# Loads in halves, a norm in VectorE's gaps, and the residual's squares moved into the attention block

## The chip, the cores and the metric

The kernel runs on one core of a Trainium2 chip. The metric is the device time in microseconds (us); lower is better. A core has five engines that run side by side and wait for one another through semaphores: TensorE (PE, matmuls and transposes), VectorE (DVE), ScalarE (ACT), GpSimd (POOL) and SyncE (SP), which here only issues DMAs. TensorE reads SBUF and writes PSUM; the others take its results from PSUM.

## The reference

One inference step of a one-layer hybrid decoder, for a prompt of 512 tokens and 64 sample tokens (8 sequences of 8), so NT = 576 tokens of D = 1024 features, all in float32:

```
h = h + mixer(rmsnorm(h))          # gated delta rule (4 heads) beside a chunked spatial gate (4 groups)
h = h + mem_attend(rmsnorm(h))     # attention of 4 heads over 256 memory rows
h = h + peer(rmsnorm(h))           # 8 heads choose 16 of 16384 experts for each token
y = rmsnorm(h)
rmsnorm(x) = x * rsqrt(mean(x*x) + 1e-6) * g
```

The mixer projects the normalised tokens with `w_in` (1024 x 3080): q, k and v go through a causal convolution of four taps and SiLU, q and k are scaled to unit length; the value rows of the spatial gate (`gv`) go through GELU and a layer norm over the 128 channels of each of 4 groups; two columns per head give the gates beta and g = -exp(a_log) * softplus(a + dt_bias). The normalised value rows of the sample tokens are also an output.

## The kernel before

Activations lie feature-major: `hT` is 128 partitions x 8 slices k x 576 tokens, the residual. Weights come in tiles of 128 output columns (128 x 8 x 128). Each float32 product is made from three products of split operands: ScalarE copies the rounded high part of a weight tile (`split_high`, L194), POOL subtracts for the low part (`split_low`, L200), and TensorE runs 8 x 3 x 2 matmuls of 288 columns (`products`, L212). The program is a sequence of blocks; at a block's end all engines meet in a barrier. The order inside a block is the order in which each engine's instructions are written.

**Input block** (`mixer_inputs`). SyncE issues eight slices of `hT`, then the constants `cst`, gains and small weights and the first three weight tiles, on one queue. ScalarE squares the slices (L113), TensorE sums the squares over the partitions with a matrix of ones out of `cst` (L121), ScalarE takes the root (L129), VectorE the reciprocal (L136) and then the scaled slices (L138), which ScalarE and VectorE split. All six small loads share one semaphore, `loaded`. Then a list `ITEMS` sets the order on TensorE and ScalarE: 24 weight tiles, with eight `l2` items (sums of squares of q and k), the gates' small matmuls (`ab`) and transposes (`turn`) put between. At tile x ScalarE first splits tile x + 1 and then takes tile x out of PSUM. For each `l2` item VectorE runs a reciprocal and a scaling (L447, L448). After the eighth come the value rows' mean, difference, square and sum (L453 to L457, `ln_vars`), ScalarE's root (`ln_roots`), three passes over the value rows (L460 to L462, `ln_done`), and the gates' functions, which ScalarE takes up behind its last tile (L393 to L402). SyncE stores the sample's value rows and waits for that store.

**Attention block** (`memory_attention`). Its last part multiplies by `w_mo`: eight tiles, m = QUERY to 4*KT - 1; VectorE adds each tile to the residual (L1468, `added`).

**Expert-score block** (`peer_scores`). It begins with squares, sums, root and reciprocal over the new residual (L113, L121, L129, L136), then the scaled slices (L138) and their splits (L1709, L1710 on ScalarE, L1744, L1747 on VectorE), for which the first tile of `peer_wq` waits slice by slice.

Of the kernel before, what the change touches and what calls it, by code (L numbers as in the profile page):

```python
# [230 lines left out]
def mixer_inputs(nc, io, sem, hT, cst, gains, rows, ps, cT, zT, vv, gate):  # L231

    with ExitStack() as ctx:
# [18 lines left out]
        h_loaded, loaded = sem("in_h_loaded"), sem("in_loaded")  # L252
# [29 lines left out]
        def _(sp):  # L282
            for k in range(KT):
                sp.dma_start(hT[:, k, :], io["xT"][:, k, :]).then_inc(h_loaded, 16)
            sp.dma_start(cst[:, :], io["consts"]).then_inc(loaded, 16)
            sp.dma_start(gains[:, :], io["gains"]).then_inc(loaded, 16)
            sp.dma_start(wab[:, :, :], w_in[:, :, 2048:2056]).then_inc(loaded, 16)
            for m in range(3):
                tiles.load(sp, m, w_in[:, :, COLS[m]:COLS[m] + P])
            sp.dma_start(cw[:, :, :], io["conv_w"]).then_inc(loaded, 16)  # L290
# [17 lines left out]
        def _(pe):  # L308
            pe.wait_ge(loaded, 96)
# [6 lines left out]

# [22 lines left out]
        def _(act):  # L339
            chain = Chain(act, act_seq)  # L340
            act.wait_ge(h_loaded, 16 * KT)
            norm_squares(act, hT, nT, squares)
            act.wait_ge(loaded, 96)
# [4 lines left out]
            act.wait_ge(zeroed, 1)  # L348

# [8 lines left out]
            for i, (kind, x) in enumerate(ITEMS):  # L358
# [31 lines left out]
                if kind == "tile" and 1 <= x <= QKV_TILES:  # L390
                    silu(x - 1)
            act.wait_ge(ln_vars, 1)
            act.activation(st[:, 1, :], st[:, 1, :], ACT.Sqrt, bias=cst[:, C_EPS:C_EPS + 1],  # L393
                           scale=1.0 / P).then_inc(ln_roots, 1)

            act.wait_ge(gate_exp_in, 1)
            act.activation(gw[:, 1, :], gw[:, 1, :], ACT.Exp)
            act.activation(rows[:, R_ALOG:R_ALOG + 4], rows[:, R_ALOG:R_ALOG + 4], ACT.Exp)
            act.activation(gw[:, 3, :].rearrange("p (i h) -> p i h", h=4), gate[:, :, 0:4],
                           ACT.Sigmoid).then_inc(gate_exps, 1)  # L400
            act.wait_ge(gate_ln_in, 1)
            act.activation(gw[:, 2, :], gw[:, 2, :], ACT.Ln).then_inc(gate_lns, 1)  # L402

        @block.vector
        def _(dve):
# [4 lines left out]
            dve.wait_ge(h_loaded, 16 * KT)  # L410
            dve.wait_ge(loaded, 96)
# [3 lines left out]
            norm_scale(dve, chain, gains, G_MIX, hT, NT, rstd[:, 0], nT, roots, normed,  # L415
                       lambda k: split_input_low(dve, nT, nhi, nlo, high, low, k))
# [27 lines left out]

            for m in range(8):
# [4 lines left out]

            v3 = vv[:, :, :].rearrange("p i (g c) -> p (i g) c", g=4)
            sqv = nT[:, :, :].rearrange("p k n -> p (k n)")[:, 0:20 * P].rearrange("p (i c) -> p i c", i=20)
            chain.after(dve.tensor_reduce(st[:, 0, :], v3, AX, ALU.add))  # L453
            chain.after(dve.tensor_scalar(st[:, 0, :], st[:, 0, :], 1.0 / P, None, ALU.mult))
            chain.after(dve.tensor_tensor(v3, v3, last(st[:, 0, :].unsqueeze(2), P), ALU.subtract))
            chain.after(dve.tensor_tensor(sqv, v3, v3, ALU.mult))
            dve.tensor_reduce(st[:, 1, :], sqv, AX, ALU.add).then_inc(ln_vars, 1)  # L457
# [667 lines left out]
def memory_attention(nc, io, sem, hT, cst, gains, ps):  # L1125
# [8 lines left out]
    with ExitStack() as ctx:  # L1134
# [38 lines left out]
        sample_out = sem("at_sample_out")  # L1173
# [50 lines left out]
        def _(pe):  # L1224
# [108 lines left out]

            for m in range(QUERY, 4 * KT):
                if m >= QUERY + 4:
                    pe.wait_ge(added, m - QUERY - 3)
                tiles.products(pe, m, ps, m % 4, nhi, nlo)

        @block.scalar
        def _(act):  # L1340
# [60 lines left out]
            for m in range(QUERY + 2, 4 * KT):  # L1401
                tiles.split_high(act, m)
# [195 lines left out]
def peer_scores(nc, io, sem, hT, cst, gains, ps, xhi, xlo, scores, gather, found, early):  # L1598

    with ExitStack() as ctx:  # L1600
# [47 lines left out]

        @block.tensor
        def _(pe):  # L1650
            norm_sums(pe, cst, nT, ps, NT, squares, sums)

            def products(m):
                if m >= 2:
# [868 lines left out]
```

## Time and profile before

| | us |
|---|---|
| median of three runs (lowest, highest) | 2122.05 (2119.13, 2127.99) |
| the profiled execution | 2121.11 |
| its span, first to last instruction | 2119.2 |
| TensorE busy | 1931.1 (91% of the span) |
| VectorE busy | 1427.9 (67%) |
| ScalarE busy | 886.3 (42%) |
| POOL busy | 768.0 (36%) |
| mean granted TensorE clock | 0.955 of full speed |

Durations below come from the profiled execution. A row of a timeline merges like instructions that follow one another (x8: eight of them); "[idle before <-releaser]" tells how long the engine had been idle and what ended it. Rows whose engine has a q (SPq) are a queue's DMA issues.

### The profile page before, as it was taken

The page shows a single profiled execution, that of the slowest core. Times are in us where ns is not written, and L with a number is a line of the kernel's source. Part 1 is how long each engine was busy: PE and PEld are TensorE (multiplying, and loading weights), DVE is VectorE, ACT ScalarE, POOL GpSimd, SP SyncE. Part 2 cuts the span into 40 slices and gives each one's busy share as a digit, 9 for nine tenths or more (in the row PEclk, how much of TensorE's full clock was granted, in tenths as well). Part 3 has the DMA queues.
Part 4 walks back from the last instruction along what each step waited for, and adds up shares of the span by engine and source line. Part 5 has one row for each costly group of instructions (what it writes and reads, how often), then busy time and mean ns, then how long its engine had stood idle before and what let it go on. Part 6 is the DMA issues. An engine that isn't in the chain of part 4 may idle for free. (4 is left out here: it accounts for less than half of the span.)

```text
span 2119.2 us, 29569 instructions
## 1 busy us (share of the span) xinstructions
PE 1931.1 (91%) x11347; PEld 1770.1 (84%) x11347; DVE 1427.9 (67%) x2554; ACT 886.3 (42%) x1765; POOL 768.0 (36%) x438
## 2 busy tenths in 40 slices
PE   4999679877898997999998999999979999999998
PEld 3999679767896696889998999999957888777777
DVE  3686554642313214998999999955568898888885
ACT  3356212213422114334444999944433343333333
POOL 0233133222530022166775455578712132222210
PEclk9899889878999999999999999999989999999999
DMA  4232101023552313269998799999999999999993
GB/s 126 63 81 60 48 1 31 1 95 89 174 189 84 131 31 80 75 196 350 378 382 325 304 372 373 374 409 403 397 347 392 394 390 400 401 400 401 400 392 115
DMA packets 211163, 511.42 MB, mean 241 GB/s; under 512 B 13264, under 2 KB 143056, under 8 KB 174160
## 3 DMA queue, kind: packets, MB, share of 16 engines
q1 hardware_dynamic: 172720, 258.65, 35.7%
q0 software_dynamic: 27648, 201.34, 23.7%
q10 hardware_dynamic: 10656, 49.55, 5.8%
q8 instruction: 91, 1.49, 0.3%
q14 instruction: 48, 0.39, 0.1%
HBM read 450.48 MB, written 59.02 MB: 240 GB/s over the span
## 5 line engine op out<-in xcount | busy, mean ns | idle before, releaser
L1891 POOL TENSOR_TENSOR ex_first_ulo<-ex_first_u,ex_first_uhi 128x1024 fp32r<-128x1024 f32 x127 | 304.7, 2400 | 207.3 <-ACT ex_first_uhi L1922 103.5
L2010 PE MATMUL ps<-xhi,ex_first_uhi 128*128 128x384 f32 x1024 | 352.7, 344 | 8.2 <-PEq L1600 4.9
L2010 PE MATMUL ps<-xlo,ex_first_uhi 128*128 128x384 f32 x1024 | 344.2, 336 | 0.0
L2010 PE MATMUL ps<-xhi,ex_first_ulo 128*128 128x384 f32 x1024 | 344.1, 336 | 0.0
L1514 POOL DMA_INDIRECT ga_ring<-in_uv,ga_idx x138 | 164.0, 1189 | 310.4 <-DVE found L1540 175.4
L2309 PE MATMUL ps<-po_vhi,po_whi 128*128 128x512 f32 x768 | 240.4, 394 | 31.3 <-DVE po_wlo L2365 15.8
L2309 PE MATMUL ps<-po_vlo,po_whi 128*128 128x512 f32 x768 | 238.4, 392 | 0.0
L2309 PE MATMUL ps<-po_vhi,po_wlo 128*128 128x512 f32 x768 | 237.7, 391 | 0.0
L2010 PEld LDWEIGHTS ps<-xhi,ex_first_uhi 128*128 128x128 f32 x1024 | 193.9, 189 | 9.1 <-issue 5.1
L2309 PEld LDWEIGHTS ps<-po_vhi,po_whi 128*128 128x128 f32 x768 | 143.8, 189 | 67.8 <-issue 22.2
L2010 PEld LDWEIGHTS ps<-xlo,ex_first_uhi 128*128 128x128 f32 x1024 | 194.0, 189 | 0.0
L2010 PEld LDWEIGHTS ps<-xhi,ex_first_ulo 128*128 128x128 f32 x1024 | 193.6, 189 | 0.0
L2309 PEld LDWEIGHTS ps<-po_vlo,po_whi 128*128 128x128 f32 x768 | 145.3, 189 | 30.8
L2309 PEld LDWEIGHTS ps<-po_vhi,po_wlo 128*128 128x128 f32 x768 | 145.1, 189 | 30.6
L1922 ACT CAST ex_first_uhi<-ex_first_u 128x1024 fp32r<-128x1024 f32 x127 | 132.5, 1043 | 69.0 <-DMA ex_first_u<-in_uT 62.8
L200 POOL TENSOR_TENSOR at_w_lo<-at_w_raw,at_w_hi 128x1024 fp32r<-128x1024 f32 x32 | 77.0, 2408 | 226.1 <-ACT at_w_hi L194 226.1
L2274 ACT CAST po_vhi<-po_v 128x1024 fp32r<-128x1024 f32 x64 | 66.7, 1044 | 190.8 <-DMA po_v<-in_peer_v 174.3
L1521 DVE CUSTOM_DVE_ANT_0 ga_ring<-ga_ring,ps 128x1024 f32<-128x1024 f32 x74 | 89.9, 1216 | 51.8 <-DMA ga_ring<-in_uv,ga_idx 51.6
L1540 DVE SCALAR_TENSOR_TENSOR ps<-ga_ring,ga_weight,ps 128x1024 f32<-128x1024 f32 x92 | 118.1, 1284 | 6.7 <-ACT ga_weight L1529 6.6
L2347 DVE TENSOR_TENSOR po_vlo<-po_v,po_vhi 128x1024 fp32r<-128x1024 f32 x64 | 78.2, 1221 | 58.5 <-ACT po_vhi L2274 58.2
L212 PE MATMUL ps<-at_nlo,at_w_hi 128*128 128x256 f32 (+1 forms) x512 | 106.0, 299 | 12.5 <-POOL at_w_lo L200 7.1
L200 POOL TENSOR_TENSOR in_w_lo<-in_w_raw,in_w_hi 128x1024 fp32r<-128x1024 f32 x24 | 59.0, 2460 | 158.0 <-ACT in_w_hi L194 158.0
(414 smaller groups left out, 4239.9 us busy)
## 6 DMA issues: line engine op xcount, KB each, us to landing
ex_first_u<-in_uT SPq DMA_DIRECT2D x128, 512.0 KB, 7.5
scores<-in_peer_v SPq DMA_DIRECT2D x32, 1024.0 KB, 9.9
po_v<-in_peer_v SPq DMA_DIRECT2D x32, 1024.0 KB, 11.9
gates<-scores ACTq DMA_DIRECT2D x12, 2048.0 KB, 12.1
scores<-gates SPq DMA_DIRECT2D x32, 768.0 KB, 15.9
acts<-ex_h ACTq DMA_DIRECT2D x62, 384.0 KB, 8.1
scores<-acts SPq DMA_DIRECT2D x31, 768.0 KB, 12.7
in_w_raw<-in_w_in SPq DMA_DIRECT2D x24, 512.0 KB, 4.0
```

What stands on the lines that cost most here:

```text
L200: pool.tensor_tensor(self.lo[m % 2], self.raw[:, m % 3], self.hi[m % 2].bitcast(F32), ALU.subtract).then_inc(self.low, 1)
L212: mm = pe.matmul(ps[:, 2 * slot + bank, 0:size], w[m % 2][:, k, :], x[:, k, c:c + size], start=(k == 0 and n == 0), stop=(k == KT - 1 and ...
L1514: pool.indirect_dma_start(self.slots[n % self.SLOTS], None, io["uv"][:, :], bass.IndirectOffsetOnAxis(ap=self.idx[:, n:n + 1], axis=0)).th ...
L1521: dve.tensor_tensor_reduce(out=self.u(n), in0=self.u(n), in1=x, op0=ALU.mult, op1=ALU.add, scale=1.0, scalar=0.0, accum_out=self.dot[:, n: ...
L1540: ins = dve.scalar_tensor_tensor(out=acc, in0=self.v(n), scalar=self.weight[:, n:n + 1], in1=acc, op0=ALU.mult, op1=ALU.add)
L1891: pool.tensor_tensor(ulo[:, j % 3], u[:, j % 3], uhi[:, j % 3].bitcast(F32), ALU.subtract).then_inc(low, 1)
L1922: act.copy(uhi[:, j % 3], u[:, j % 3]).then_inc(high, 1)
L2010: mm = pe.matmul(ps[:, j % 2, 0:ND], w[:, j % 3, k, :], x[:, k, :], start=(k == 0 and n == 0), stop=(k == KT - 1 and n == 2))
L2274: act.copy(vhi[:, e % 4], v(e)).then_inc(v_high, 1)
L2309: mm = pe.matmul(ps[:, 2 * t + a, :], x[:, s, e % 4, t * P:(t + 1) * P], y[:, e % 4, a * 512:(a + 1) * 512], start=(e == 0 and n == 0), st ...
L2347: dve.tensor_tensor(vlo[:, e % 4], v(e), vhi[:, e % 4].bitcast(F32), ALU.subtract).then_inc(v_low, 1)
```

## The change

Three parts.

**Start.** `hT` comes in two halves of four slices, each with a semaphore of its own, and the constants stand between the halves. TensorE waits for the constants alone; the small loads not needed until later are waited for later (`loaded` at 64). ScalarE runs one small Sqrt before the sums are there.

**Value rows.** VectorE's mean, difference, square and sum stand between the scalings m = 3 to 6, ScalarE's root of the variances behind the `l2` item 7, and its gate functions behind tiles 20 and 22.

**Residual.** In the last part of the attention block ScalarE squares each new slice of the residual, and TensorE sums the squares behind the tile after the next; the expert-score block starts with the root. The weight tiles use three PSUM pairs instead of four.

```diff
+            for half in range(2):
+                for k in range(4 * half, 4 * half + 4):
+                    sp.dma_start(hT[:, k, :], io["xT"][:, k, :]).then_inc(h_loaded[half], 16)
+                if half == 0:
+                    sp.dma_start(cst[:, :], io["consts"]).then_inc(cst_loaded, 16)
+            sp.dma_start(gains[:, :], io["gains"]).then_inc(gains_loaded, 16)
...
         def _(pe):
-            pe.wait_ge(loaded, 96)
+            pe.wait_ge(cst_loaded, 16)
             norm_sums(pe, cst, nT, ps, NT, squares, sums)
...
+            act.wait_ge(cst_loaded, 16)
+            act.activation(gw[:, 3, 0:1], cst[:, C_EPS:C_EPS + 1], ACT.Sqrt)
             norm_root(act, cst, ps, NT, rstd[:, 0], sums, roots)
...
+                if (kind, x) == ("l2", 7):
+                    act.wait_ge(ln_vars, 1)
+                    act.activation(st[:, 1, :], st[:, 1, :], ACT.Sqrt, bias=cst[:, C_EPS:C_EPS + 1],
+                                   scale=1.0 / P).then_inc(ln_roots, 1)
+                elif (kind, x) == ("tile", 20):
+                    act.wait_ge(gate_exp_in, 1)
+                    act.activation(gw[:, 1, :], gw[:, 1, :], ACT.Exp)
+                    act.activation(rows[:, R_ALOG:R_ALOG + 4], rows[:, R_ALOG:R_ALOG + 4], ACT.Exp)
+                    act.activation(gw[:, 3, :].rearrange("p (i h) -> p i h", h=4), gate[:, :, 0:4],
+                                   ACT.Sigmoid).then_inc(gate_exps, 1)
+                elif (kind, x) == ("tile", 22):
+                    act.wait_ge(gate_ln_in, 1)
+                    act.activation(gw[:, 2, :], gw[:, 2, :], ACT.Ln).then_inc(gate_lns, 1)
...
+                if m == 3:
+                    dve.wait_ge(taken, place["turn", 2] + 1)
+                    chain.after(dve.tensor_reduce(st[:, 0, :], v3, AX, ALU.add))
+                    chain.after(dve.tensor_scalar(st[:, 0, :], st[:, 0, :], 1.0 / P, None, ALU.mult))
+                elif m == 4:
+                    chain.after(dve.tensor_tensor(v3, v3, last(st[:, 0, :].unsqueeze(2), P), ALU.subtract))
+                elif m == 5:
+                    chain.after(dve.tensor_tensor(sqv, v3, v3, ALU.mult))
+                elif m == 6:
+                    dve.tensor_reduce(st[:, 1, :], sqv, AX, ALU.add).then_inc(ln_vars, 1)
...
+            def residual_sums(k):
+                pe.wait_ge(new_squares, k + 1)
+                for a in range(2):
+                    pe.matmul(ps[:, 6 + a, 0:HALF], cst[:, C_ONES:C_ONES + P], qT[:, k, a * HALF:(a + 1) * HALF],
+                              start=(k == 0), stop=(k == KT - 1))
+
             for m in range(QUERY, 4 * KT):
-                if m >= QUERY + 4:
-                    pe.wait_ge(added, m - QUERY - 3)
-                tiles.products(pe, m, ps, m % 4, nhi, nlo)
+                if m >= QUERY + 3:
+                    pe.wait_ge(added, m - QUERY - 2)
+                tiles.products(pe, m, ps, (m - QUERY) % 3, nhi, nlo)
+                if m >= QUERY + 2:
+                    residual_sums(m - QUERY - 2)
+            for k in range(KT - 2, KT):
+                residual_sums(k)
...
-            norm_squares(act, hT, nT, squares)
+            act.activation(rstd.rearrange("p (a n) -> p a n", a=2), ps[:, 6:8, 0:HALF], ACT.Sqrt,
+                           bias=cst[:, C_EPS:C_EPS + 1], scale=1.0 / D).then_inc(roots, 1)
             tiles.split_high(act, 0)
-            norm_root(act, cst, ps, NT, rstd, sums, roots)
```

The SyncE queue at the start of the input block. Before:

```order
L284 DMA hT<-in_xT 128x576 x8
L285 DMA cst<-in_consts 128x2313
L286 DMA gains<-in_gains 128x41
L287 DMA in_wab<-in_w_in 128x8x8
L187 DMA in_w_raw<-in_w_in 128x8x128 x3
```

And now:

```order
L286 DMA hT<-in_xT 128x576 x4
L288 DMA cst<-in_consts 128x2313
L286 DMA hT<-in_xT 128x576 x4
L289 DMA gains<-in_gains 128x41
L187 DMA in_w_raw<-in_w_in 128x8x128 x3
L292 DMA in_wab<-in_w_in 128x8x8
```

The constants moved ahead of four slices of the residual; `in_wab` moved behind the weight tiles.

ScalarE in the input block from the last `l2` item (the first row) on. Before:

```order
L373 ACTIVATE in_rstd<-ps,cst 128x576 [waits in_made]
L194 CAST in_w_hi<-in_w_raw 128x1024 [waits in_w_used,in_w_loaded0]
L389 ACT_TABLE_LOAD
L389 ACTIVATE zT<-ps 128x576 [waits in_w_used]
L194 CAST in_w_hi<-in_w_raw 128x1024 [waits in_w_used,in_w_loaded1]
```

And now:

```order
L380 ACTIVATE in_rstd<-ps,cst 128x576 [waits in_made]
L402 ACTIVATE in_st<-in_st,cst 128x20 [waits in_ln_vars]
L194 CAST in_w_hi<-in_w_raw 128x1024 [waits in_w_used,in_w_loaded0]
L396 ACT_TABLE_LOAD
L396 ACTIVATE zT<-ps 128x576 [waits in_w_used]
L406 ACT_TABLE_LOAD
L406 ACTIVATE in_gw<-in_gw 128x20 [waits in_gate_exp_in]
L407 ACTIVATE rows<-rows 128x4
L408 ACT_TABLE_LOAD
L408 ACTIVATE in_gw<-gate 128x20
L194 CAST in_w_hi<-in_w_raw 128x1024 [waits in_w_used,in_w_loaded1]
```

The root of the variances now stands ahead of the split of tile 21, and two table loads with three small activations ahead of the split of tile 22.

ScalarE across the barrier between the attention block and the expert-score block. Before:

```order
L194 CAST at_w_hi<-at_w_raw 128x1024 [waits in_w_used,in_w_loaded1]
L1134 UNCONDITIONAL_BRANCH
L1701 UNCONDITIONAL_BRANCH [waits barrier_Pool_Activation_PE_DVE_SP_release]
L113 ACTIVATE ga_ring<-hT 128x576 x8
L194 CAST ps_w_hi<-ps_w_raw 128x1024 [waits in_ln_done]
L129 ACT_TABLE_LOAD
L129 ACTIVATE ga_x<-ps,cst 128x576 [waits ou_w_loaded2]
```

And now (some semaphore names are those of earlier blocks, whose numbers are used again):

```order
L1432 ACTIVATE at_qT<-hT 128x576 [waits dl_wS_loaded] x3
L1433 ACT_TABLE_LOAD
L1433 ACTIVATE at_small<-cst 128x1
L1150 UNCONDITIONAL_BRANCH
L1730 UNCONDITIONAL_BRANCH [waits barrier_Pool_Activation_PE_DVE_SP_release]
L1732 ACTIVATE ga_x<-ps,cst 128x576
L194 CAST ps_w_hi<-ps_w_raw 128x1024 [waits in_gate_lns]
```

Squares and table load moved ahead of the barrier, and the root is the first instruction behind it.

## Rows read from the trace of the kernel before

**Rows 1.** Timeline, start: start us, length us, engine, line, tiles, count [idle before <-releaser].

```profile
0.75 3.72 SPq L284 DMA_DIRECT2D hT<-in_xT  x8
...
4.51 0.57 SPq L285 DMA_DIRECT2D cst<-in_consts  x1
...
9.97 4.69 ACT L113 ACTIVATE in_nT<-hT 128x576 f32<-128x576 f32 x8 [7.95 <-DMA hT<-in_xT]
...
21.33 11.04 PE L121 MATMUL ps<-in_nT,cst 128*128 128x288 f32 x32 [21.33 <-DMA rows<-in_rows]
...
32.45 1.28 ACT L129 ACT_TABLE_LOAD   x1 [17.79 <-PE ps L121]
```

**Rows 2.** Windows at the start: stretch, busy per engine, granted clock, DMA share, GB/s.

```profile
0.00:9.97 9.97, 0.00 (x0) 0.00 (x0) 0.52 (x3) 1.28 (x1) 0.20 (x4) 1.00 0.82 292
...
9.97:12.20 2.23, 0.00 (x0) 0.00 (x0) 0.00 (x0) 2.23 (x4) 0.00 (x0) 1.00 1.03 327
```

**Rows 3.** Timeline of VectorE between two of the eight scalings.

```profile
175.71 0.76 DVE L448 SCALAR_TENSOR_TENSOR cT<-cT,in_rstd 128x576 f32<-128x576 f32 x1
...
178.72 3.75 DVE L447 RECIPROCAL in_rstd<-in_rstd 128x576 f32<-128x576 f32 x1 [2.26 <-ACT in_rstd L373]
```

**Rows 4.** Timeline of VectorE, first operation of the value rows' norm.

```profile
205.29 2.81 DVE L453 TENSOR_REDUCE in_st<-vv 128x20 f32<-128x2560 f32 x1
```

**Rows 5.** Timeline of ScalarE, last tiles of the input projection and what follows.

```profile
205.45 0.65 ACT L389 ACTIVATE zT<-ps 128x576 f32<-128x576 f32 x1 [2.42 <-PE ps L212]
...
224.65 0.65 ACT L389 ACTIVATE zT<-ps 128x576 f32<-128x576 f32 x1 [5.75 <-PE ps L212]
...
225.32 1.28 ACT L393 ACT_TABLE_LOAD   x1
...
226.62 0.31 ACT L393 ACTIVATE in_st<-in_st,cst 128x20 f32<-128x20 f32 x1
```

**Rows 6.** Timeline of VectorE in the convolution.

```profile
139.22 2.98 DVE L426 SCALAR_TENSOR_TENSOR cT<-in_pre,in_cw,cT 128x512 f32<-128x512 f32 x1
...
142.43 0.75 DVE L426 SCALAR_TENSOR_TENSOR cT<-in_pre,in_cw,cT 128x512 f32<-128x512 f32 x1
```

**Rows 7.** Timeline of POOL, the splits of two weight tiles.

```profile
139.26 2.39 POOL L200 TENSOR_TENSOR in_w_lo<-in_w_raw,in_w_hi 128x1024 fp32r<-128x1024 f32 x1 [4.01 <-ACT in_w_hi L194]
...
213.52 4.00 POOL L200 TENSOR_TENSOR in_w_lo<-in_w_raw,in_w_hi 128x1024 fp32r<-128x1024 f32 x1 [4.01 <-ACT in_w_hi L194]
```

**Rows 8.** Timeline of the SyncE queue, end of the input block.

```profile
235.84 0.57 SPq L299 DMA_DIRECT2D out_vrows<-vv  x1
```

**Rows 9.** Timeline of TensorE, start of the recurrent block.

```profile
238.65 2.05 PE L621 MATMUL ps<-cst,gate 128*128 128x128 f32 x8 [14.03 <-PEq L233]
...
245.40 1.06 PE L621 MATMUL ps<-cst,gate 128*128 128x128 f32 x8
```

**Rows 10.** Timeline of TensorE, a sum between two weight tiles.

```profile
197.89 1.13 PE L327 MATMUL ps<-in_nT,cst 128*128 128x288 f32 x4
...
198.64 0.65 PE L212 MATMUL ps<-in_nhi,in_w_hi 128*128 128x288 f32 x2
```

**Rows 11.** Timeline of VectorE, end of attention and start of the expert-score block.

```profile
799.37 0.76 DVE L1468 TENSOR_TENSOR hT<-hT,ps 128x576 f32<-128x576 f32 x1 [5.64 <-PE ps L212]
...
812.68 3.75 DVE L136 RECIPROCAL ga_x<-ga_x 128x576 f32<-128x576 f32 x1 [11.15 <-ACT ga_x L129]
...
828.74 0.69 DVE L1753 COPY ps_nS<-ga_ring 128x1024 f32<-128x1024 f32 x1
```

**Rows 12.** Timeline of ScalarE, first operation of the expert-score block.

```profile
801.42 4.69 ACT L113 ACTIVATE ga_ring<-hT 128x576 f32<-128x576 f32 x8 [13.74 <-PEq L2404]
```

**Rows 13.** DMA issues of the expert-score block: KB each, median us to landing.

```profile
ps_w_raw<-in_peer_wq SPq DMA_DIRECT2D x8, 512.0 KB, 4.3
```

**Rows 14.** Windows: small matmuls of the gates, and the last attention tiles (columns of Rows 2).

```profile
55.00:60.00 5.00, 5.00 (x25) 5.00 (x25) 0.72 (x5) 0.00 (x0) 0.00 (x0) 0.50 0.01 4
...
751.00:799.00 48.00, 48.00 (x361) 48.00 (x361) 5.28 (x7) 6.30 (x6) 14.35 (x6) 1.00 0.12 33
```

More of the change, by code:

```diff
@@ L250, in mixer_inputs @@
         tiles = SplitTiles(nc, ctx, sem, "in_")
-        h_loaded, loaded = sem("in_h_loaded"), sem("in_loaded")
+        h_loaded, loaded = [sem(f"in_h_loaded{i}") for i in range(2)], sem("in_loaded")
+        cst_loaded, gains_loaded = sem("in_cst_loaded"), sem("in_gains_loaded")
         squares, sums, roots, normed = sem("in_squares"), sem("in_sums"), sem("in_roots"), sem("in_normed")
@@ L340, in _ @@
             chain = Chain(act, act_seq)
-            act.wait_ge(h_loaded, 16 * KT)
-            norm_squares(act, hT, nT, squares)
-            act.wait_ge(loaded, 96)
+            for k in range(KT):
+                if k % 4 == 0:
+                    act.wait_ge(h_loaded[k // 4], 64)
+                act.activation(nT[:, k, :], hT[:, k, :], ACT.Square).then_inc(squares, 1)
+            act.wait_ge(cst_loaded, 16)
+            act.activation(gw[:, 3, 0:1], cst[:, C_EPS:C_EPS + 1], ACT.Sqrt)
             norm_root(act, cst, ps, NT, rstd[:, 0], sums, roots)
@@ L409, in _ @@
             dve.memset(gate[:, 4, :], 0.0).then_inc(zeroed, 1)
-            dve.wait_ge(h_loaded, 16 * KT)
-            dve.wait_ge(loaded, 96)
+            for i in range(2):
+                dve.wait_ge(h_loaded[i], 64)
+            dve.wait_ge(gains_loaded, 16)
+            norm_scale(dve, chain, gains, G_MIX, hT, NT, rstd[:, 0], nT, roots, normed,
+                       lambda k: split_input_low(dve, nT, nhi, nlo, high, low, k))
+            dve.wait_ge(loaded, 64)
             for b in range(2):
@@ L1400, in _ @@
                     mix_high(i - 2)
-            for m in range(QUERY + 2, 4 * KT):
-                tiles.split_high(act, m)
+            for m in range(QUERY + 2, 4 * KT + 2):
+                if m < 4 * KT:
+                    tiles.split_high(act, m)
+                k = m - QUERY - 2
+                act.wait_ge(added, k + 1)
+                act.activation(qT[:, k, :], hT[:, k, :], ACT.Square).then_inc(new_squares, 1)
+            act.activation(small[:, 0, 0, 0:1], cst[:, C_EPS:C_EPS + 1], ACT.Sqrt)
         @block.vector
@@ L1611, in peer_scores @@
         kbd = sb("kbd", [P, PH, 2 * NKEY])
-        squares, sums, roots, normed = sem("ps_squares"), sem("ps_sums"), sem("ps_roots"), sem("ps_normed")
+        roots, normed = sem("ps_roots"), sem("ps_normed")
         taken, low, g_high, g_low = sem("ps_taken"), sem("ps_low"), sem("ps_g_high"), sem("ps_g_low")
@@ L1650, in _ @@
         def _(pe):
-            norm_sums(pe, cst, nT, ps, NT, squares, sums)
             def products(m):
```

34 lines of the change are left out of this document (7 added, 27 removed).

## The prediction, made before the changed kernel was run

> **What bounds the kernel now.** I read the busy shares first, then the timelines of the three places that the change touches, then what each engine waits for there. TensorE is busy 91% of the span, but at each of the three places it stands idle, and there the path goes through other engines, so that time taken out of them comes off the span. (1) At the start the squares are ready when ScalarE has worked from 9.97 to 14.66 us, yet TensorE begins the sums at 21.33, when the last small load lands; ScalarE loads a table after the sums [rows 1]. (2) The input block's last tile leaves PSUM at 225.3; TensorE comes back at 238.65, having waited for the value rows' norm on VectorE and the store behind it [rows 5, 8, 9]. (3) From the last addition of attention (799.37) to the reciprocal of the next norm (812.68) TensorE has nothing but the sums [rows 11, 12]. What follows a place waits for the block that ends there, so I carry a shift on to the end; the DMA-bound expert stages start from these blocks too.
>
> **Part 1, the start.** By 9.97 us the queue had moved 9.97 x 292 = 2.91 MB, though the eight slices, which had then landed, are 2.36 MB; by 12.2, when the constants (1.18 MB) were in, 3.64 MB [rows 2]. Now four slices and the constants are the first 2.36 MB. Taking the same count, the constants land at about 10.0 and the last four slices at 12.2. Bounds for the constants: 8.4 (2.36 MB alone at that pace from the first packet) and 12.2 (behind everything). The squares of the first half are long done. The sums take 11.04 us for eight slices [rows 1], 5.5 for the first four, so that the second four are asked for at 15.5; their squares are done at 12.2 + 2.4 = 14.6. The sums end at 21.0 instead of 32.4: -11.3, with bounds -12.9 and -9.1. The table load (1.28) falls into the wait of ScalarE: -1.3. The root, the reciprocal, the split of tile 0 and the slices follow as before. Part 1: **-12.6** (-14.2 to -10.4).
>
> The trace shows that load directly followed by its activation: it begins at 225.32 and the activation at 226.62 [rows 5]. The Trainium skill ("ScalarE: Activation LUTs", What ACT_TABLE_LOAD costs) adds a drain of about 1.38 us to each switch; by that the preload would give 1.4 us more here, and each load that part 2 puts ahead of a weight split would cost 1.4 more. The row shows no such gap, and I go by the row.
>
> **Part 2, the value rows.** What goes: the tail behind 225.3. The new end is ScalarE's last SiLU plus the barrier. The barrier is bounded by 0, since the store issued at 235.84 and the barrier take 2.8 together [rows 8, 9], and 1.3 (799.37 + 0.76 to 801.42) [rows 11, 12]; I take 0.8. What is late next is the tiles themselves, since ScalarE and VectorE work now stands between them.
>
> VectorE has 2.26 us free between two scalings [rows 3]. Behind m = 3 come a reduction of 2.81 [rows 4] and a short operation (0.2): 0.8 over. The difference and the square (as long as the reduction) and the second reduction keep that lag, so the variances are ready at about 201.8 and ScalarE, free at 200.8, splits tile 21 one microsecond late. Its low part comes at 205.7, against a start of tile 21 at 205.3: 0.4 us of stall. Behind tile 20 (SiLU from 205.45 [rows 5]) stand two table loads of 1.28 and three small activations, 3.2 us together; the split of tile 22 is then done at 210.3 and POOL (2.39) at 212.8. TensorE asks for it at 205.4 + 6.4 = 211.8: 1.0 us of stall in all.
>
> But POOL and VectorE hold each other up. A VectorE step of 0.75 took 2.98 when it started just before POOL's split (139.22 against 139.26), and a split of 2.39 took 4.00 at 213.52, where VectorE was squaring value rows [rows 6, 7]. Both VectorE steps read two SBUF operands. In the new order the split of tile 22 is ready at 210.3 while VectorE multiplies value rows by the gain, until 212.5; POOL would end at 214.9 and tile 22 start 3.1 us late. Tile 23 has room. Bounds of the stall: 0.5 (POOL slips between) and 4.5 (both last tiles caught); I take 3.0. TensorE then returns at 224.65 + 3.0 + 0.65 + 0.8 = 229.1: -9.5 against 238.65. It comes back after some 4.5 us instead of 14. Its first eight matmuls took 2.05 us, the same eight later 1.06 [rows 9], and with the three groups behind them ScalarE got its rows about 1.4 us later than at full clock: -1.4 (bounds 0 and -1.5). Part 2: **-10.9** (-14 to -7.5).
>
> The Trainium skill ("SBUF — State Buffer", Who interferes with whom) names this an exclusive lock, held for a whole instruction, against VectorE operations with two SBUF inputs. By the rows alone I could not exclude that only part of the time is lost; by that rule it is all of it, and the free case below drops out.
>
> **Part 3, the residual.** Added in the attention block: a sum for each slice costs TensorE 0.75 us between tiles (197.89 to 198.64) [rows 10]. Six stand before the last tile's end: +4.5. The seventh lies beside the last addition. Behind that addition ScalarE has a square (0.6, an eighth of 4.69), the table load (1.28) and a small activation (0.3): +2.2; the eighth sum lies beside them. So the next block starts 6.7 us later. Three PSUM pairs instead of four cost nothing: the addition (0.76) is over more than a tile before its pair is used again. Taken away in the next block: the reciprocal stood 812.68 - 801.42 = 11.26 us behind the first instruction [rows 11, 12]; the root alone puts it 0.85 behind: -10.4.
>
> What then comes late is the first weight tiles: they take 4.3 us to land [rows 13], which the squares had hidden. ScalarE splits the first at about 4.2 to 5.2 and the second at 5.6 to 6.6, so POOL's two splits (2.39 each) run while VectorE goes through its chain of scalings and subtractions, 12.3 us long (about 816.45 to 828.74, busy throughout [rows 11]), all of them with two SBUF operands. Before, both were over when it began. If every microsecond is lost as in rows 6 and 7, that is +4.8, and I take it. Part 3: 6.7 - 10.4 + 4.8 = **+1.1** (-3.7 without collision, +2 with the wait for the second tile on top).
>
> **Sum.** -12.6 - 10.9 + 1.1 = -22.4. Against the profiled execution's 2121.1 that is 2098.7; the median before lies 0.9 above it, so 2099.6, and I say **2099**.
>
> **Rivals.** *A, no collisions*: POOL slips into gaps, -12.6 - 13.3 - 3.7 = -29.6: 2092. For it: rows 7 also show full-speed splits; against it, long VectorE steps stand back to back in both places. *B, half a start*: the constants land with or behind the last slices (12.2), and both of the last tiles are caught: -10.4 - 7.5 + 2 = -16: 2106. For it, 0.55 MB of other transfers had already moved when the slices landed; against it, the queue still finished in the order of issue. *C, given back later*: the shift changes how the later stages fall, say the granted clock in the recurrent block, and two fifths of the gain are left: 2113, no change that can be told. Against it, nothing in those stages is tied to a time from the start. *D, the sums cool TensorE*: while TensorE ran the gates' 80 small matmuls, of 8 columns, its clock fell to half, 1.2 GHz [rows 14]. If the float32 sums between the attention tiles do the same from the first sum on, six tiles of 6.4 us take double: +38, and the kernel comes to 2138, slower. It decides from about four tiles at half clock (+26). Against it, the sum of rows 10 has the same 288 columns as the new ones and took 0.75 us, with the tiles around it at full pace. *E, the norm in the gaps holds the tiles up as much as the tail cost*, so that part 2 does not do what it says: -12.6 - 1.4 + 1.1 = -12.9, 2109; against it, the gaps are there in rows 3.
>
> **How the numbers follow.** Forecast 50%, A 20%, B 14%, E 5%, C 8%, D 3%. A measurement of this kernel can tell about 0.5%, 10.6 us: faster means below 2111.4, slower above 2132.7. Forecast, A, B and E are faster, 89%, of which 1% goes over the bound at their outer edge; with C that makes 9% the same, and D is slower: faster 0.88, same 0.09, slower 0.03. The range takes A's centre with 3 us of its own and B and E: 2089 to 2110.
>
> **What the changed profile would show.** Sums from about 10.0 to 21.0 us, and the first weight product near 28.8 instead of 41.39. Times below are less that shift: the split of tile 22 by POOL longer than 2.39 or late, TensorE idle about 3 us around tiles 21 and 22, its return some 4.5 us behind the last tile. A scaling at m = 4 about 0.8 us behind its root. Tiles of 7.15 us instead of 6.4 in the attention's last part, at full clock; the root first in the next block, the reciprocal 0.85 behind it; POOL's two first splits or VectorE's steps beside them stretched by about 4.8 together. I am wrong on part 1 if the sums start after 12.2, on part 2 if TensorE's return moves by less than 7, on part 3 if the chain of VectorE ends earlier than before relative to the attention's last tile by more than 1 us.

## The result, and the profile after

| | before | after |
|---|---|---|
| median, us (lowest, highest) | 2121.92 (2119.13, 2127.99), 4 runs | 2100.84 (2096.24, 2103.27), 4 runs |
| span of the profiled execution | 2119.2 | 2094.3 |
| mean granted TensorE clock | 0.955 | 0.954 |

The ratio is 0.9887, with a 95% interval of 0.9857 to 0.9917: faster by 21.1 us in the medians, 24.0 by the ratio, and 24.9 in the two profiled spans. Forecast were 2099 and a range of 2089 to 2110. Below, "shift" is the time of an instruction in the trace of before less that of the same instruction after. The "first product" is TensorE's first matmul of a weight tile, the "return" its first matmul of the recurrent block, and the "chain's last copy" the copy on VectorE that ends the scaling chain of the expert-score block (L1753 before, L1782 after).

**The start.** Timeline of the kernel after, all engines (columns as in [rows 1]):

```profile
2.62 0.43 SPq L288 DMA_DIRECT2D cst<-in_consts  x1
...
7.52 2.40 ACT L347 ACTIVATE in_nT<-hT 128x576 f32<-128x576 f32 x4 [5.50 <-DMA hT<-in_xT]
13.39 2.40 ACT L347 ACTIVATE in_nT<-hT 128x576 f32<-128x576 f32 x4 [3.46 <-DMA hT<-in_xT]
15.81 1.28 ACT L349 ACT_TABLE_LOAD   x1
17.10 0.20 ACT L349 ACTIVATE in_gw<-cst 128x1 f32<-128x1 f32 x1
21.20 0.74 ACT L129 ACTIVATE in_rstd<-ps,cst 128x576 f32<-128x576 f32 x1 [3.90 <-PE ps L121]
...
10.35 10.82 PE L121 MATMUL ps<-in_nT,cst 128*128 128x288 f32 x32 [10.35 <-DMA cst<-in_consts]
28.95 0.82 PE L212 MATMUL ps<-in_nhi,in_w_hi 128*128 128x288 f32 x2 [7.79 <-DVE in_nlo L227]
```

The constants land between the two halves, and ScalarE's table load (1.28 us) stands inside the time in which it waits for the sums; in [rows 1] it stood behind them. A window of the kernel after, with the columns of [rows 2]:

```profile
0.00:10.35 10.35, 0.00 (x0) 0.00 (x0) 0.51 (x3) 3.68 (x5) 0.20 (x4) 1.00 0.82 284
```

10.35 x 284 is 2.94 MB moved when the constants were in, against 2.91 by which the prediction placed them.

**The last tiles of the input block.** Timelines of the kernel after: VectorE, POOL, ScalarE, TensorE.

```profile
192.01 2.83 DVE L476 TENSOR_TENSOR vv<-vv,in_st 128x2560 f32<-128x2560 f32 x1
...
197.73 4.86 DVE L478 TENSOR_TENSOR vv<-vv,rows 128x2560 f32<-128x2560 f32 x1
202.51 2.35 DVE L481 TENSOR_SCALAR in_gw<-in_gw 128x20 f32<-128x20 f32 x1
...
188.69 2.40 POOL L200 TENSOR_TENSOR in_w_lo<-in_w_raw,in_w_hi 128x1024 fp32r<-128x1024 f32 x1 [5.86 <-ACT in_w_hi L194]
196.27 8.56 POOL L200 TENSOR_TENSOR in_w_lo<-in_w_raw,in_w_hi 128x1024 fp32r<-128x1024 f32 x2 [5.18 <-ACT in_w_hi L194]
...
191.45 0.65 ACT L396 ACTIVATE zT<-ps 128x576 f32<-128x576 f32 x1 [1.53 <-PE ps L212]
192.12 1.28 ACT L406 ACT_TABLE_LOAD   x1
...
193.74 1.28 ACT L408 ACT_TABLE_LOAD   x1
...
195.16 1.03 ACT L194 CAST in_w_hi<-in_w_raw 128x1024 fp32r<-128x1024 f32 x1
...
208.22 0.65 ACT L396 ACTIVATE zT<-ps 128x576 f32<-128x576 f32 x1 [8.73 <-PE ps L212]
...
214.62 0.65 ACT L396 ACTIVATE zT<-ps 128x576 f32<-128x576 f32 x1 [2.91 <-PE ps L212]
...
200.05 0.57 PE L212 MATMUL ps<-in_nhi,in_w_hi 128*128 128x288 f32 x2 [2.18 <-POOL in_w_lo L200]
...
215.58 1.13 PE L637 MATMUL ps<-cst,gate 128*128 128x128 f32 x8 [0.99 <-PEq L233]
```

The two splits of POOL, tiles 22 and 23, take 8.56 us together where one alone takes 2.40, and TensorE waits 2.18 us for the first of them. From the SiLU of tile 20 (191.45) to the last (214.62) there are 23.17 us, where three tiles of 6.4 are 19.2: the tiles were held up by 4.0 us, not by 2.2. Most of the rest is in the clock (windows of the kernel after, columns of [rows 2]):

```profile
196.00:200.00 4.00, 1.87 (x15) 1.63 (x13) 3.96 (x2) 3.06 (x4) 3.73 (x2) 1.00 0.00 0
200.00:203.30 3.30, 3.25 (x15) 3.28 (x16) 3.30 (x2) 0.00 (x0) 3.30 (x1) 0.55 0.02 5
```

Right behind the wait the granted clock was 0.55 for 3.3 us, near its lower level of 1.2 GHz. From tile 22's first matmul (200.05) to its SiLU (208.22) there are 8.17 us where a tile at 2.4 GHz takes 6.4: 1.8 us lost besides the wait, about 1.5 of them by the clock (3.3 x 0.45). The return (215.58) follows the last SiLU by 0.96 us, where 14.0 lay between them in [rows 5, 9], and the eight first small matmuls take 1.13 instead of 2.05.

**The residual.** Timelines of the kernel after: TensorE between two attention tiles, then VectorE, ScalarE, POOL at the end of attention.

```profile
767.60 1.13 PE L1353 MATMUL ps<-at_qT,cst 128*128 128x288 f32 x4
768.36 0.65 PE L212 MATMUL ps<-at_nhi,at_w_hi 128*128 128x288 f32 x2
768.84 0.42 PE L212 MATMUL ps<-at_nlo,at_w_hi 128*128 128x288 f32 x2
...
775.16 0.75 DVE L1499 TENSOR_TENSOR hT<-hT,ps 128x576 f32<-128x576 f32 x1 [6.61 <-PE ps L212]
782.52 0.76 DVE L1499 TENSOR_TENSOR hT<-hT,ps 128x576 f32<-128x576 f32 x1 [6.61 <-PE ps L212]
...
787.55 3.75 DVE L136 RECIPROCAL ga_x<-ga_x 128x576 f32<-128x576 f32 x1 [0.66 <-ACT ga_x L1732]
791.34 6.46 DVE L138 SCALAR_TENSOR_TENSOR ga_ring<-hT,gains,ga_x 128x576 f32<-128x576 f32 x3
...
807.80 0.68 DVE L1782 COPY ps_nS<-ga_ring 128x1024 f32<-128x1024 f32 x1
...
786.77 0.74 ACT L1732 ACTIVATE ga_x<-ps,cst 128x576 f32<-128x576 f32 x1 [1.27 <-PEq L2433]
790.73 1.04 ACT L194 CAST ps_w_hi<-ps_w_raw 128x1024 fp32r<-128x1024 f32 x1 [3.22 <-DMA ps_w_raw<-in_peer_wq]
...
791.86 5.32 POOL L200 TENSOR_TENSOR ps_w_lo<-ps_w_raw,ps_w_hi 128x1024 fp32r<-128x1024 f32 x2 [2.41 <-ACT ps_w_hi L194]
```

The tiles are 7.36 us apart (782.52 - 775.16) instead of 6.4. The reciprocal stands 0.78 behind the block's first instruction, where it stood 11.26 behind it in [rows 11, 12]. Behind it three scalings take 6.46 us beside POOL's first two splits, where they take 2.27 alone. In the attention's last tiles the clock stayed full:

```profile
730.00:780.00 50.00, 50.00 (x361) 48.95 (x360) 5.28 (x7) 10.50 (x13) 14.40 (x6) 1.00 0.12 32
```

**The shift along the span.** First product 12.44 (41.39 to 28.95); return 23.07; chain's last copy 20.94 (828.74 to 807.80); end 24.9. Between the places of the change the shift drifts by itself, from 23.1 to 27.6 us in the recurrent block and from 25.5 to 21.7 in the attention, as bursts of half clock come and go.

### The profile page after: what moved, and what is told of

It reads as the page before. It is cut to its first block and busy times, and to the rows that moved or that the text cites. A ratio compares the mean times of both kernels' runs of the same rounds, so it can differ in the third digit from the quotient of the medians.

```text
span 2094.3 us, 29576 instructions
## 1 busy us (share of the span) xinstructions
PE 1930.1 (92%) x11347; PEld 1770.4 (85%) x11347; DVE 1437.7 (69%) x2554; ACT 887.8 (42%) x1768; POOL 771.5 (37%) x438
## 5 line engine op out<-in xcount | busy, mean ns | idle before, releaser
L2039 PEld LDWEIGHTS ps<-xhi,ex_first_uhi 128*128 128x128 f32 x1024 | 194.0, 189 | 10.9 <-issue 6.9
L1983 ACT ACTIVATE ex_h<-ps 128x384 f32<-128x384 f32 x124 | 60.1, 485 | 140.1 <-PE ps L2039 138.0
L212 PE MATMUL ps<-at_nlo,at_w_hi 128*128 128x256 f32 (+1 forms) x512 | 107.1, 301 | 12.6 <-POOL at_w_lo L200 7.2
## 6 DMA issues: line engine op xcount, KB each, us to landing
scores<-acts SPq DMA_DIRECT2D x31, 768.0 KB, 12.2
```

What stands on the lines that cost most here:

```text
L212: mm = pe.matmul(ps[:, 2 * slot + bank, 0:size], w[m % 2][:, k, :], x[:, k, c:c + size], start=(k == 0 and n == 0), stop=(k == KT - 1 and ...
L1983: act.activation(dst, ps[:, (j - 1) % 2, 0:ND], ACT.Gelu_apprx_tanh).then_inc(gelus, 1)
L2039: mm = pe.matmul(ps[:, j % 2, 0:ND], w[:, j % 3, k, :], x[:, k, :], start=(k == 0 and n == 0), stop=(k == KT - 1 and n == 2))
```

## Experiments

The kernels were timed in three groups, each on another chip and beside the kernel before: 2121.15 us with the first four below, 2121.57 with the next three and the constants behind both halves, 2124.08 with the other three. So kernels of different groups are compared by their ratios, which all are to the kernel before.

### The start alone

```diff
+                if half == 0:
+                    sp.dma_start(cst[:, :], io["consts"]).then_inc(cst_loaded, 16)
...
+            act.activation(gw[:, 3, 0:1], cst[:, C_EPS:C_EPS + 1], ACT.Sqrt)
```

> Part 1 alone on the kernel before. Theory (the start is worth what its own waits were): first weight product at 28.9 us instead of 41.4, about 13 us less in all, near 2109. Rival (a good part of the 21 us came from elsewhere, say a better granted clock after the start): less than 9 us.

Measured: 2104.30 us (2101.11 to 2111.13), ratio 0.9921 (0.9892 to 0.9950), so 16.8 us faster (10.6 to 22.9). The expected 13 lies in that interval, the rival's "less than 9" does not. TensorE's timeline in this kernel:

```profile
10.05 10.96 PE L121 MATMUL ps<-in_nT,cst 128*128 128x288 f32 x32 [10.05 <-DMA cst<-in_consts]
28.80 0.82 PE L212 MATMUL ps<-in_nhi,in_w_hi 128*128 128x288 f32 x2 [7.79 <-DVE in_nlo L227]
```

The first product is the predicted 28.8. The return (224.44) and the chain's last copy (814.00) are 14.2 and 14.7 us sooner than before: about 2 more than the start itself gives, picked up behind the first product.

One trace on each side doesn't fix the gain, because the sums themselves last longer or shorter. In all thirteen traces of this case the first 6 to 13 of their 32 matmuls stand about 0.48 us apart and the others 0.24, so that the eight sums take from 9.41 to 11.04 us without a pause. The earliest first product with this start is that of a kernel further below, with the exponentials moved and the operand in PSUM:

```profile
9.59 9.70 PE L121 MATMUL ps<-in_nT,cst 128*128 128x288 f32 x32 [9.59 <-DMA cst<-in_consts]
27.08 0.82 PE L212 MATMUL ps<-in_nhi,in_w_hi 128*128 128x288 f32 x2 [7.79 <-DVE in_nlo L227]
```

Nine traces with the new start have it at 27.08 to 29.02, 28.23 on the mean; the three with the old one at 39.83, 40.86 and 41.39, 40.69 on the mean. The start gives 12.5 us.

### The value rows alone

```diff
+                elif m == 4:
+                    chain.after(dve.tensor_tensor(v3, v3, last(st[:, 0, :].unsqueeze(2), P), ALU.subtract))
...
+                elif (kind, x) == ("tile", 20):
+                    act.wait_ge(gate_exp_in, 1)
```

> Part 2 alone on the kernel before. Theory: TensorE returns 9 to 10.5 us earlier after the input block, though tile 22 starts some 4 us late; about 2112. Rival (the norm in the gaps gives back what the tail cost, and the gain was part 1's): within 3 us of the kernel before.

Measured: 2115.39 us (2105.93 to 2120.76), ratio 0.9970 (0.9953 to 0.9987), 6.4 us faster (2.8 to 10.0), where 9 to 10.5 were expected. TensorE:

```profile
213.52 0.50 PE L212 MATMUL ps<-in_nhi,in_w_hi 128*128 128x288 f32 x2 [2.19 <-POOL in_w_lo L200]
```

The same wait as in the kernel after, so it is this part's own. The return (229.04) is 9.6 us sooner than before, 0.5 of which the first product (40.86) had already; the chain's last copy is 8.05 sooner. The rival, a gain within 3 us, is out by the trace; by the times alone it would not quite be.

### The residual alone

```diff
+                if m >= QUERY + 2:
+                    residual_sums(m - QUERY - 2)
...
+                act.activation(qT[:, k, :], hT[:, k, :], ACT.Square).then_inc(new_squares, 1)
```

> Part 3 alone on the kernel before. Theory (five sums and the end chain add 7.0 us ahead of the barrier, the shorter head takes 10.5 away, POOL's splits give 4.2 back): the last VectorE subtraction of the expert-score block moves by +0.7 us, the time by less than 2 us, near 2123. Rival (the 10.4 us of the head come off): 2118 or lower.

Measured: 2121.92 us (2116.76 to 2135.24), ratio 1.0009 (0.9986 to 1.0033). The shift is 3.2 us ahead of the part's first sum and 2.8 at the chain's last copy: 0.3 us lost. So the rival with a real gain is out. Together the three ratios give -16.8 - 6.4 + 1.9 = -21.3 us, the three medians -21.8; the kernel after has -24.0 by its ratio and -21.1 in its medians. Within the intervals, each 7 to 13 us wide, the parts add.

### The gates' exponentials behind the cast of tile 22

```diff
+                    if x == 21:
+                        act.wait_ge(gate_exp_in, 1)
...
-                elif (kind, x) == ("tile", 20):
```

> The changed kernel with ScalarE's exponentials and sigmoid of the gates moved from behind tile 20's SiLU to behind the split of tile 22. Theory (the split of tile 22 is late because of the 3.2 us ahead of it on ScalarE, and then caught by VectorE's pass): POOL's split of tile 22 starts at about 194.9, TensorE does not wait at tile 22, and 3.5 to 4 us go: near 2097. Rival (the collision with VectorE alone decides): the split still takes over 3.5 us and TensorE waits as before, 2101.

Measured: 2096.59 us (2093.72 to 2102.46), ratio 0.9886 (0.9858 to 0.9913). POOL in this kernel (tiles 22, 23), then ScalarE's SiLUs of tiles 20 and 23:

```profile
193.67 3.97 POOL L200 TENSOR_TENSOR in_w_lo<-in_w_raw,in_w_hi 128x1024 fp32r<-128x1024 f32 x1 [2.03 <-ACT in_w_hi L194]
200.11 2.46 POOL L200 TENSOR_TENSOR in_w_lo<-in_w_raw,in_w_hi 128x1024 fp32r<-128x1024 f32 x1 [2.46 <-ACT in_w_hi L194]
...
192.01 0.65 ACT L402 ACTIVATE zT<-ps 128x576 f32<-128x576 f32 x1 [1.52 <-PE ps L212]
...
211.25 0.65 ACT L402 ACTIVATE zT<-ps 128x576 f32<-128x576 f32 x1 [2.92 <-PE ps L212]
```

From tile 20 to the last there are 19.24 us, against 23.17: all of the hold-up is gone, although the split of tile 22 still takes 3.97. Without ScalarE's lateness there is no hold-up; the collision costs only on top of it. The 3.9 us are in the trace; the ratio (0.9886 against 0.9887) doesn't show them.

### VectorE's passes behind the split of tile 22

```diff
+            dve.wait_ge(tiles.low, 23)
```

> The kernel after, with one wait more: VectorE's three passes over the values (192.01 to 202.5) wait until POOL has split tile 22's low half (196.27, 3.64 us). Theory: tile 22 is late for two reasons, ScalarE's gate exponentials with their function loads ahead of its cast (about 1.0 us of lateness), and VectorE and POOL holding each other up on the tile (POOL's split 3.6 to 4.0 us where it takes 2.4 alone, 1.2 to 1.6 us). With the wait the split of tile 22 takes 2.4 us and ends near 198.7, and TensorE waits about 1.0 us in place of 2.2; VectorE's passes end about 4 us later, near 206.5, which is still ahead of the last SiLU (214.6), so nothing else moves: the time is 1 to 2.5 us below the kernel after. Rival (all of the lateness is ScalarE's, the ports cost nothing): POOL's split starts at the same 196.3 and its length does not change, TensorE waits the same 2.2 us and the time is the same. Second rival: the passes, now beside tile 23's split, hold that one up instead, and the wait moves by one tile: the time is the same with the wait at tile 23.

Measured: 2100.98 us (2096.74 to 2111.01), ratio 0.9901 (0.9876 to 0.9926). The split of tile 22 on POOL, TensorE's wait for it, and the last SiLU:

```profile
196.31 2.37 POOL L200 TENSOR_TENSOR in_w_lo<-in_w_raw,in_w_hi 128x1024 fp32r<-128x1024 f32 x1 [5.18 <-ACT in_w_hi L194]
...
198.83 0.50 PE L212 MATMUL ps<-in_nhi,in_w_hi 128*128 128x288 f32 x2 [0.92 <-POOL in_w_lo L200]
...
211.89 0.65 ACT L396 ACTIVATE zT<-ps 128x576 f32<-128x576 f32 x1 [0.54 <-PE ps L212]
```

The wait goes from 2.18 to 0.92, as the theory has it: 1.0 is ScalarE's, 1.2 the collision's. But the last SiLU comes 2.7 us sooner, twice what the wait lost: behind the shorter wait the stretch from tile 22's first matmul to its SiLU takes 6.66 us, behind the longer one 8.17. The split of tile 23 took 4.56 us here, and TensorE did not wait for it: the second rival is out. The expected gain of 1 to 2.5 us is not in the times (ratio 0.9901 against 0.9887). In the profiled run, the slowest of the six (2111.01), it is there until the chain's last copy (804.19), and then the rest of the program takes 1304.9 us, where it takes 1286.5 in the kernel after and up to 1297.8 in the others.

### The scaling operand in PSUM

```diff
-            norm_scale(dve, chain, gains, G_FFN, hT, NT, rstd, nT, roots, normed, lows)
+            half = ps[:, 6:8, 0:HALF]
+            chain.after(dve.reciprocal(half, rstd.rearrange("p (a n) -> p a n", a=2)))
...
+                                         scalar=gains[:, G_FFN + k:G_FFN + k + 1], in1=half,
```

> The kernel after, with the reciprocal root of the residual's norm and the operand of its eight scalings in the PSUM banks 6 and 7, so that a scaling on VectorE reads one operand from SBUF in place of two. Theory: the collision in the residual's scaling chain (three scalings at 6.46 us where they take 2.28 alone, POOL's splits 5.32 where they took 2.4 to 4.0, chain end 4.2 us later than the moved start alone would give) comes from two SBUF inputs of VectorE's instruction beside POOL. With one SBUF input the scalings go at about 2.3 to 2.8 us beside POOL, POOL's splits at 2.4 to 4.0, and the chain of eight ends 2 to 4 us sooner (last copy of the chain at 804 to 806 in place of 807.8): the time is 2 to 4 us below the kernel after. Rival (VectorE and POOL exclude each other whatever VectorE reads from): the scalings stay at 6.4 us, and the time is the same within 1 us. Second rival: an instruction with a PSUM operand is itself slower by a bit, and that takes the gain back: scalings at 2.9 us or more with no POOL beside them.

Measured: 2098.97 us (2095.54 to 2099.94), ratio 0.9889 (0.9867 to 0.9912). VectorE and POOL in this kernel:

```profile
788.85 3.76 DVE L1782 RECIPROCAL ps<-ga_x 128x576 f32<-128x576 f32 x1 [0.66 <-ACT ga_x L1732]
792.64 2.27 DVE L1784 SCALAR_TENSOR_TENSOR ga_ring<-hT,gains,ps 128x576 f32<-128x576 f32 x3
795.53 0.60 DVE L1773 TENSOR_TENSOR xlo<-ga_ring,xhi 128x384 fp32r<-128x384 f32 x1 [0.62 <-ACT xhi L1738]
796.05 2.56 DVE L1776 TENSOR_TENSOR ps_glo<-ga_ring,ps_ghi 128x256 fp32r<-128x256 f32 x1
...
807.79 0.69 DVE L1792 COPY ps_nS<-ga_ring 128x1024 f32<-128x1024 f32 x1
...
793.35 4.98 POOL L200 TENSOR_TENSOR ps_w_lo<-ps_w_raw,ps_w_hi 128x1024 fp32r<-128x1024 f32 x2 [2.61 <-ACT ps_w_hi L194]
```

With one operand in PSUM three scalings take 2.27 us beside POOL's splits, not 6.46: what collided was their second SBUF input. Of the 4.2 us saved the chain keeps 1.3 (18.94 us from the reciprocal to the copy, against 20.25). The first subtraction now waits 0.62 us for ScalarE, whose casts stand behind its two weight casts, and the next step with two SBUF inputs, a subtraction of 0.41, takes 2.56. The theory held for the cause; of its 2 to 4 us the trace shows 1.3, and the ratio none (0.9889 against 0.9887).

### Both edits together, and all three

> The kernel after with two edits together: ScalarE's gate exponentials behind its cast of tile 22 (which alone came to 2096.6 against 2100.8), and the residual's scaling operand in PSUM. If each is right by itself, and since they lie 500 us apart and touch nothing in common, they add: 4 us for the first and 2 to 4 us for the second, 2093 to 2095. If the operand in PSUM is worth nothing (the rival of the run with that edit alone), 2096 to 2097.

Measured: 2096.80 us (2089.97 to 2111.26), ratio 0.9899 (0.9869 to 0.9929). The expected 2093 to 2095 was missed: the two gains did not add in the times. The profiled run is the fastest of the six (span 2088.0), and it shows what such differences are worth. Against the kernel with the exponentials moved alone, this one is 0.9 us ahead at the return and 9.1 at 730 us, with no edit between the two. Two windows of TensorE there, in the kernel with the exponentials moved alone and then in this one (stretch, busy, granted clock, DMA share, GB/s):

```profile
620.00:630.00 10.00, 7.39 (x27) 0.75 0.00 0
...
720.00:730.00 10.00, 8.82 (x46) 0.66 0.01 2
```

```profile
620.00:630.00 10.00, 7.39 (x41) 1.00 0.00 0
...
720.00:730.00 10.00, 10.00 (x77) 1.00 0.18 52
```

The same instructions met these two bursts of half clock in one run, and a third between 680 and 700 us (0.82 and 0.84), and none in the other.

The third edit (the wait of VectorE's passes) on top, and beside it the kernel after once more:

> The kernel after with three edits: the gate exponentials behind the cast of tile 22, VectorE's three value passes behind POOL's split of tile 22, and the residual's scaling operand in PSUM. Theory: with the exponentials moved alone, the split of tile 22 took 3.97 us beside the passes and TensorE lost nothing; with the passes waiting it takes 2.4 and TensorE waits for nothing either, so the last edit adds nothing at tile 22, and the last SiLU comes 3.4 us sooner than in the kernel after (near 211.3); the scaling chain gives 1.2. About 4 to 5 us in all below the kernel after, near 2096. Rival: the passes, later now, end after the last SiLU's neighbours and delay the value rows' store or the recurrent block's first operand; then the return is 1 to 3 us later and the gain is half.

> The kernel after, unchanged, run beside the two below so that they are compared on one chip. Theory: near 2101, as in its first timing (2096.2 to 2103.3); its first product at 28.95 and its residual's root near 787, and what lies behind the root differs by several us from run to run, because the last 900 us keep the transfers at their limit.

Measured side by side: 2099.43 us (2097.93 to 2104.35), ratio 0.9884 (0.9862 to 0.9906), and for the kernel after 2102.45 (2099.73 to 2110.14), ratio 0.9904 (0.9879 to 0.9929): 3.0 us apart in the medians, where 4 to 5 were expected, with overlapping intervals. POOL's split of tile 22 takes 2.39 and TensorE waits for none, but the last SiLU (211.48) is no sooner than with the exponentials moved alone (211.25): the rival's delay did not appear, and the last edit adds nothing, as expected. The four versions so far with the exponentials moved, the operand in PSUM, or both have medians 1.4 to 4.3 us below the kernel after's 2100.84, but ratios of 0.9884 to 0.9899 against its 0.9887 and 0.9904; so that one of them beats it is likely from the traces and not shown by the times.

### The constants behind both halves

```diff
-                if half == 0:
-                    sp.dma_start(cst[:, :], io["consts"]).then_inc(cst_loaded, 16)
+            sp.dma_start(cst[:, :], io["consts"]).then_inc(cst_loaded, 16)
```

> The kernel after with the constants' load issued behind both halves of the first input, in place of between them. Theory: the first sums wait for the constants (10.35 in the kernel after, where the squares of the first half are done at about 9.8), and the transfers share the engines, so the constants last land when about all 3 MB have moved, near 12.4 to 12.9 by the rate of the first window; the sums then start at 12.4 to 13, but they end with the squares of the second half anyway (13.39 and on), and TensorE's sums (10.82 us for the eight of them at this clock) become the longer chain: the root 2 to 2.5 us later, first product near 31 in place of 28.95, the time 2 to 2.5 us above the kernel after (near 2103). Rival (the halves' own semaphores give all of it, and the place of the constants nothing): sums still start near 10.4, and the time is the same.

Measured: 2104.24 us (2096.72 to 2105.45), ratio 0.9912 (0.9887 to 0.9937). TensorE:

```profile
13.02 9.41 PE L121 MATMUL ps<-in_nT,cst 128*128 128x288 f32 x32 [13.02 <-DMA cst<-in_consts]
30.21 0.82 PE L212 MATMUL ps<-in_nhi,in_w_hi 128*128 128x288 f32 x2 [7.79 <-DVE in_nlo L227]
```

The sums start 2.7 us later than in the kernel after (2.8 later than the mean of the nine traces with the constants between the halves, 9.59 to 10.71). The first product comes only 1.26 us later, because the sums take 9.41 us here and 10.82 there. That is no merit of the order: their matmuls follow one another without a pause in both, and in kernels with the same start as after's they took 9.70 to 10.96. Against the nine first products given above, 30.21 is 1.2 to 3.1 us later, 2.0 on the mean, near the 2 to 2.5 expected; the rival, with sums still starting near 10.4, is out. So of the 12.5 us of the start about 2 come from the place of the constants in the queue, and about 10.5 from TensorE and ScalarE waiting for what they need alone (with the table load).

### The exponentials moved, the residual's part left out

```diff
-                if m >= QUERY + 2:
-                    residual_sums(m - QUERY - 2)
```

> The kernel after without its third part (the residual's squares and sums stay in the next block, as before), and with the gate exponentials behind the cast of tile 22. Theory: the third part is worth nothing in sum (its run alone came to 2121.9 against 2121.2, and the milestones give 0.3 to 0.7 us against it), so this is at the time of the kernel after with the same exponentials edit, 2096.6, within 2 us. Rival (the third part helps or hurts once the others are in): over 3 us off that.

Measured: 2102.92 us (2087.58 to 2105.17), ratio 0.9883 (0.9852 to 0.9914). The ratio is that of the kernel with the exponentials moved and the residual's part in (0.9886). In the traces, with the same granted clock between 600 and 700 us, the return and the chain's last copy are 592.7 us apart here (211.90 to 804.62) and 593.3 there (212.20 to 805.50): the part costs 0.6 us (0.8 by the shift just ahead of it). The median is 6 us off, which is the rival's case by its words, but before was 3 us slower in this group too.

## Why the prediction came out right

The forecast of 2099 and the 2100.84 measured lie closer together than the record can tell apart: the stretch behind the scaling chain alone takes from 1286.5 to 1304.9 us. In the times the parts alone missed in opposite directions, the start with -16.8 where -12.6 was forecast (inside its interval), the value rows with -6.4 where -10.9 was (just outside it). That the sum hit so well is partly luck; what bears it are the steps in the traces.

**Part 1** was right in its steps. Sums from 10.35 to 21.17 (10.0 to 21.0 forecast), the load hidden, the first product 12.44 sooner, 12.5 on the means (12.6 forecast). What I had wrong is the credit: I argued from the order of the queue, and the order is worth about 2 us. With the constants last they land at 13.02, later than my bound of 12.2, and the sums still end at 22.43, 9.9 sooner than before, where my bound for that case was -9.1; that is by their 9.41 us, where I had 11.04. The Trainium skill's drain of about 1.38 us at a switch ("ScalarE: Activation LUTs", What ACT_TABLE_LOAD costs) is not borne out: the load begins 0.02 us behind the square before it (15.79 to 15.81), and the activation 1.29 us after the start of a load that itself takes 1.28 (15.81 to 17.10).

**Part 2** came to -10.3 by the trace of the value rows alone (-9.1 for the return behind the first product, -1.2 for the warm clock) against -10.9. One pair is not exact here either: the return stands 195.7 to 197.3 us behind the first product in the three traces without the part, and 186.6 to 188.2 in the five with it as forecast, 8.7 less on the mean. The step "tile 22 start 3.1 us late", with its stall of 3.0, was mis-sized: it was 2.18 us of wait and 1.8 more that I did not have, mostly the clock's fall behind the wait. Against that, I had the barrier at 0.8, and the return comes 0.3 us behind the end of the last SiLU. ScalarE's lateness of 1.0 us was right (0.92 with the collision taken away), and the lag of 0.8 on VectorE too, except that it did not hold tile 21 up. The exclusive lock of the Trainium skill ("SBUF — State Buffer", Who interferes with whom) agrees with the steps of two SBUF inputs and with the freed scalings. It also counts a `tensor_scalar` that reads through both ports among the steps that collide, which is the form of the first point of the last section (2.35 us beside a split); no row here tells the port mode.

**Part 3**: +1.1 forecast; the three pairs of traces give +0.3, +0.6 and +0.7 (the last in the kernel after, 21.7 to 20.9). "A sum costs 0.75, six stand before the last tile's end: +4.5" was wrong twice and right in the sum: a sum costs 0.96, because the pair behind it takes 0.48 until the next where it otherwise takes 0.27 (768.36 to 768.84), and five stand ahead of the last tile's end: 4.8. The pair was there to be read in [rows 10], where the two matmuls behind the sum took 0.65. The collision cost 4.2 on the chain against 4.8.

**The rivals.** A (no collisions) is refuted by the POOL and VectorE rows; its 13.3 doesn't follow from my working, which gives 13.0 with the stall of 1.0 and 13.5 with the bound of 0.5. B is refuted by the start's times. D is refuted by the clock of 1.00 through the last tiles. E is out too: the return moved by 10.6 us more than the first product did (7.5 to 10.7 over all pairs). C (the shift changes the clock later) exists and is smaller than I priced it: the shift wanders by some 4 us within and between the blocks here, though by 8.2 in another pair. What stays open is why the stretch from the scaling chain to the end takes anything from 1286.5 to 1304.9 us, with a DMA share of 0.91 to 1.04 in windows of 240 to 360 us from 1200 to 2080; so a gain of 2 to 4 us ahead of it can't be followed in the medians.

## What to carry to other kernels

Give every first load a semaphore of its own before tuning the order of the queue: here the waits for "all loads" held about 10.5 us and the order about 2. When work is put into an engine's gaps, ask what the next operand of the busiest engine waits for, and put function loads behind it: two table loads ahead of one weight cast brought 4.0 us of hold-up, most of it by way of a collision and the clock. Where two engines collide, moving one operand to PSUM frees that step, but look at what then collides in its place.

## What the runs showed of the hardware beyond that

- A VectorE step can be held for POOL's whole split even when it is tiny: a 128x20 scaling by one number took 2.35 us beside a split (202.51), and 0.17 without (in the kernel with the passes behind the split). It has one tensor input, so two SBUF inputs are not the whole of the condition. The same form took 1.41 us in the kernel before (208.13) and ended with POOL's split (209.51); a reduction of 2.81 us ahead of it lost nothing beside that split.
- Scalings with one operand in PSUM ran at full speed beside POOL: 2.27 us for three, against 6.46.
- A wait of TensorE of 2.18 us cost 4.0, one of 0.92 cost 1.2 (20.40 us from the SiLU of tile 20 to the last, less 19.2): behind the longer one the granted clock was 0.55 for 3.3 us. In the four other traces with such a wait (2.17 to 2.33 us) it read 0.57 to 0.67 over the 3.2 to 4.0 us behind it.
- Bursts of half clock in stretches where TensorE is busy 74% and 88% of the time fall differently in runs with identical code there, and moved the shift by 8.2 us in one pair of traces (0.9 to 9.1).
- The same 32 matmuls of the first sums took from 9.41 to 11.04 us: 6 to 13 of them at 0.48 us each before the rest went at 0.24, while the clock column reads 1.00. What sets the moment of the change is open.
